# Expert loop: the scatter of an expert moved behind the first product of the next, the next expert's token rows moved ahead of the second product

## The reference

```
aff = softmax(h @ w_router)                       # 256 tokens x 16 experts
gate, idx = top_k(aff.T, 32)                      # each expert takes 32 tokens
xs = h[idx]                                       # (16, 32, 1024)
a = silu(xs @ w_gate) * (xs @ w_up)               # each 1024 x 1024 for an expert
out = (a @ w_down) * gate                         # 1024 x 1024
y = zeros(256, 1024).at[idx].add(out)             # added back at the tokens
```

## Time and profile before

| | |
|---|---|
| median of 3 runs | 2054.88 us (2052.83 to 2055.36) |
| profiled execution, its own time | 2058.72 us |
| span of the profiled execution | 2056.9 us |
| PE busy | 1718.2 us, 84% |
| DVE busy | 572.5 us, 28% |
| ACT busy | 416.4 us, 20% |
| moved from and to HBM | 571.73 MB, mean 278 GB/s |
| first expert stage (L1090 first to L1113 last) | 1042.0 to 1500.4 us |
| second expert stage | 1581.0 to 2038.9 us |

### The profile page before, as it was taken

One profiled execution on the slowest core, in us unless ns is written; L12 is line 12 of the kernel. 1 busy time (PEld: TensorE's weight loads), 2 busy tenths in 40 slices (PEclk: granted clock), 3 DMA queues, 4 the chain that ended last, 5 costly groups with the idle time before them and its releaser, 6 DMA issues.

```text
span 2056.9 us, 22697 instructions
## 1 busy us (share of the span) xinstructions
PE 1718.2 (84%) x9278; PEld 1084.1 (53%) x9278; DVE 572.5 (28%) x1298; ACT 416.4 (20%) x732; POOL 18.5 (1%) x26
## 2 busy tenths in 40 slices
PE   6999989999999999996878776776788886777776
PEld 4544348887888886553744333332345443343333
DVE  3243145116888536547230000000024000000002
ACT  4222241002130023212221111111123211111111
POOL 0000000000110000000000000000000000000000
PEclk8999997999999999887878889889897889889988
DMA  9425730244558835105379999999955999999995
GB/s 368 163 82 205 269 144 1 82 159 145 208 205 307 309 124 205 41 1 206 118 291 422 429 428 428 429 429 429 428 193 226 415 428 428 429 429 429 428 429 233
DMA packets 110591, 571.73 MB, mean 278 GB/s; under 512 B 9122, under 2 KB 15394, under 8 KB 85955
## 3 DMA queue, kind: packets, MB, share of 16 engines
q1 hardware_dynamic: 109488, 568.66, 68.5%
q10 hardware_dynamic: 1042, 2.24, 0.3%
HBM read 569.83 MB, written 1.05 MB: 278 GB/s over the span
## 4 chain that ended last, share of the span: by engine, by line
PE 58%; DMA 32%; DVE 5%; ACT 2%; issue 2%; SPq 1%; DVEq 0%; ACTq 0%
DMA ring<-in_w_exp_up_dram 29%; PE bank L456 19%; PE bank L1090 8%; PE bank L800 8%; PE bank L827 4%; PE bank L464 3%; PE bank L482 2%; PE bank L1152 1%; PE bank L1106 1%; PE bank L843 1%; PE bank L536 1%; DMA ring<-in_w_exp_down_dram 1%; PE bank L507 1%; PE bank L1113 1%; DMA ring<-in_w_ada_dram 1%
## 5 line engine op out<-in xcount | busy, mean ns | idle before, releaser
L1090 PE MATMUL bank<-ring,arena 128*32 128x512 f32 x2048 | 300.9, 743 | 101.7 <-DMA ring<-in_w_exp_up_dram 80.0
L1090 PEld LDWEIGHTS bank<-ring,arena 128*32 128x32 f32 x2048 | 80.7, 132 | 297.2 <-issue 243.0
L2289 DVE TENSOR_TENSOR arena<-arena,bank 128x256 f32<-128x256 f32 x32 | 13.5, 421 | 697.7 <-ACT arena L1580 697.7
L1106 PE MATMUL bank<-ring,arena 128*32 128x512 f32 x1024 | 134.3, 663 | 57.9 <-DVE arena L2289 49.2
L456 PE MATMUL bank<-ring,hT 128*128 128x512 f32 (+4 forms) x480 | 162.0, 494 | 6.5 <-issue 4.9
L800 PE MATMUL bank<-hT,ring 128*128 128x256 f32 x704 | 156.5, 385 | 4.2 <-ACT hT L1286 4.2
L800 PEld LDWEIGHTS bank<-hT,ring 128*128 128x128 f32 x704 | 135.4, 193 | 23.3 <-issue 4.6
L1113 PE MATMUL bank<-arena 128*128 (+1 forms) x512 | 118.9, 385 | 29.0 <-DVE arena L2293 29.0
L1113 PEld LDWEIGHTS bank<-arena 128*128 128x128 f32 x512 | 94.6, 190 | 69.5 <-issue 54.5
L456 PEld LDWEIGHTS bank<-ring,hT 128*128 128x128 f32 x480 | 87.5, 194 | 76.7 <-issue 66.9
L1076 PEld LDWEIGHTS bank<-arena 128*128 128x128 f32 x960 | 113.8, 194 | 1.6
(11 more groups left out here) (309 smaller groups left out, 1670.5 us busy)
## 6 DMA issues: line engine op xcount, KB each, us to landing
ring<-in_w_exp_gate_dram SPq DMA_DIRECT2D x64, 2048.0 KB, 17.6
ring<-in_w_exp_up_dram SPq DMA_DIRECT2D x64, 2048.0 KB, 22.1
ring<-in_w_exp_down_dram SPq DMA_DIRECT2D x64, 2048.0 KB, 22.4
ring<-in_w_mod_dram SPq DMA_DIRECT2D x24, 2048.0 KB, 13.5
ring<-in_w_ada_dram SPq DMA_DIRECT2D x12, 2048.0 KB, 13.3
ring<-in_w_up_dram SPq DMA_DIRECT2D x10, 2048.0 KB, 11.5
ring<-in_w_in_dram SPq DMA_DIRECT2D x8, 2048.0 KB, 14.1
ring<-in_w_down_dram SPq DMA_DIRECT2D x5, 2048.0 KB, 9.2
```

The lines of the kernel that those rows point to most:

```text
L1090: ins = pe.matmul(bank[0][32 * q:32 * q + 32, :], xe[:, k * CAP:(k + 1) * CAP], xs[q // 2][:, o:o + 512], start=(k == 0), stop=(k == KD - ...
L1106: ins = pe.matmul(bank[2 + h][32 * q:32 * q + 32, :], act_t[:, 4 * j + q, :], x[:, q, h * 512:h * 512 + 512], start=(j == 0), stop=(j == 1 ...
```

## The change

`down` is split in three: `products` (the four transposes), `down` (the down product) and `scatter`. The loop on PE is now `products(e)`, `rows(e + 1)`, `down(e)`, `gate_up(e + 1)`, `scatter(e)`. ACT's `between_products` is split in the same way, with the copy of the token rows ahead of the copy of bank 3. DVE and SP are as before, and so is the number of instructions of each kind.

```diff
-                def down(e, last=False):
+                def products(e):
+
                     pe.wait_ge(sem("gu_copied"), e + (N_EXP * layer + 1))
                     for j in range(4):
                         ins = pe.transpose(bank[1][:, j * 128:j * 128 + 128], gu[:, j * 128:j * 128 + 128], ident)
                     ins.then_inc(done, 1)
+
+                def down(e):
 
                     pe.wait_ge(sem("act_ready"), e + (N_EXP * layer + 1))
...
                     ins.then_inc(done, 1)
+
+                def scatter(e, last=False):
 
                     pe.wait_ge(sem("down_copied"), e * 2 + (2 * N_EXP * layer + 2))
...
                 with pe.Fori(0, N_EXP - 1) as e:
+                    products(e)
+                    rows(e + 1)
                     down(e)
-                    rows(e + 1)
                     gate_up(e + 1)
-                down(N_EXP - 1, last=True)
+                    scatter(e)
+                products(N_EXP - 1)
+                down(N_EXP - 1)
+                scatter(N_EXP - 1, last=True)
...
-                def between_products(e):
+                def gate_and_up(e):
                     act.wait_ge(sem("gate_up_done"), e * 2 + (2 * N_EXP * layer + 2))
...
+
+                def down_rows(e):
                     act.wait_ge(done, e * 3 + (base + 2))
                     act.copy(dsb[:, 1, :], bank[3]).then_inc(sem("down_copied"), 1)
...
                 with act.Fori(0, N_EXP - 1) as e:
-                    between_products(e)
+                    gate_and_up(e)
                     rows(e + 1)
-                between_products(N_EXP - 1)
+                    down_rows(e)
+                gate_and_up(N_EXP - 1)
+                down_rows(N_EXP - 1)
```

## The result

The changed kernel takes 2061.29 us (median of 7 runs, 2057.2 to 2064.46) against 2055.36 us for the kernel before on the same chip (7 runs, 2052.83 to 2056.44). The ratio is 1.0032 with a 95% interval of 1.0020 to 1.0044: slower by about 6 us. A second comparison, with 12 and 35 runs, gave 1.0030 (1.0017 to 1.0043). The forecast was 2054.4 us and no change, with a range that ended at 2060.

What follows compares the result with a forecast made beforehand. Transfers were taken to bound the expert loop, so only stage ends count: ramp -4.9, tails +4.7 (half clock) or +2.0 (full), branches +0.3, weighted about -0.6. Forecast median 2054.4 us, no change; range 2050.5 to 2060.

Steps and rivals of the forecast that it cites:

- Rivals 2 and 3: Inside the stages: slots, not bytes, set the period, 2032 us, chance 0.03; PE becomes the bound, +240 us, chance 0.01.
- the tail: Last landings to last scatter of each stage: scatter delays the last down product, +2.4 and +2.3 us at half clock.
- half clock at its start, 5.00 us: Tail: last gate/up half starts at half clock after a long wait and takes 5.00 us, against 3.64 at full clock.
- the ramp: Each stage's start, where PE hands back the first slots: hole before second slot 0 closes, -2.7 and -2.2, together -4.9 us.
- It just makes it; I count 0: Ramp: slot 4 goes out at 1065.7 to 1067.2, due by 1067.4; cost 0, with 0.5 us as bad end.
- rival 1: Ramp: the dry queue only moves to slot 4, token rows and down product at half clock; +11, 2066 us; chance 0.04.
- PE's path to the hand-back: Ramp, expert 0: from transposes' end at 1058.34, token rows to 1062.0, down product 3.64 to 5.15 us, end 1065.6 to 1067.1.
- The deadline: Ramp: slot 4 must land at 1055.6 + 4 x 4.9 = 1075.2, so be out by 1067.4.
- by bytes, 4.0 at the least: Ramp gain counted by bytes: first hole 2.0 us, the second scaled the same way, -4.0 us at the least.
- six pitches: Inside the stages: a pitch is one 2048 KB slot's transfer, 4.90 us at 428 GB/s; six slots, one expert, take 29.4 us.
- The alternative with the skill's 6.9 us: Ramp: a lone slot landing 6.9 us after issue would make holes of 1.0 and 1.2 us, a gain of 2.2.
- its cover in the steady expert: Steady expert: slots 4 and 5 handed back 4 to 5 us later, 12 us of cover left, so 0 us.

Runs made afterwards that it cites:

- e6: The change in rounds 1 to 13, first and last rounds with token rows behind down product and scatter between gate/up halves; 2051.95 against 2054.61 us before, ratio 0.9986.
- e5: The change plus five extra matmuls between the gate/up halves in each loop round; 2058.14 against 2054.61 us for the kernel before, ratio 1.0020.
- e8: The change plus two extra matmuls in PE's short waits ahead of the loop; 2057.26 against 2054.61 us for the kernel before, ratio 1.0006.
- e7: The changed kernel itself measured again, nothing altered; 2061.62 against 2054.61 us for the kernel before, ratio 1.0030.
- e3: The change, but the round ending with the last gate/up has the scatter ahead of it; 2059.74 against 2056.23 us for the kernel before, ratio 1.0012.
- e2: The change's scatter move alone, token rows back behind the down product and ACT's copies in old order; 2057.38 against 2056.23 us before, ratio 0.9997.
- e4: Against the kernel before: scatter moved between the gate/up halves, token rows behind the down product as before; 2051.48 against 2056.23 us, ratio 0.9978.
- e9: The change plus extra matmuls both ahead of the loop (two) and between the gate/up halves (five); ratio 0.9989 against the kernel before.

## Why the prediction was wrong

**Right:** that the transfers bind the middle, and that the ends decide. 352.4 us before and after between the same two landings, and e6, where thirteen rounds in the new order cost next to nothing. Rivals 2 and 3 (slots set the period; PE becomes the bound) are out: the rate stayed at 427 and 428 GB/s at a granted clock of 0.86 and 0.88.

**Right in kind, short in size: the tail.** Forecast +5.0 in the two stages; +6.4 in the first profile (14.9 and 14.8), +4.6 in the second (13.9 and 14.0). The step "half clock at its start, 5.00 us" took the two values shown in the earlier trace rows as the price of a long wait. The last half took 5.2 to 6.3 us in the two profiles. e5 splits the first profile's 14.9 into 12.3 with a warm half and 2.6 of clock. The rule of the Trainium skill cited in the prediction ("TensorE: Matmul & The Clock Gate", Loop structure matters more than you think), that a long wait for a DMA ahead of matmuls leaves them on a cold engine, agrees with both: 5.2 to 6.3 us behind waits of 4.5 to 6.1 us, and 3.64 with the wait filled. The length of a shorter wait did not decide it, as I had read from the earlier trace rows: in the changed kernel a gate/up half took 3.64 us behind a wait of 2.90 (at 1472.54) and 5.34 behind one of 2.93 (at 2015.39).

**Wrong: the ramp.** The failed step is the sentence on slot 4, "It just makes it; I count 0". Slot 4 went out at 20.9 us, and with it slot 5 landed 2.3 and 2.4 us later than before. It was rival 1, which had 0.04 and asked for 2 us of lateness to count as slower; 1.1 were enough. Three things in the step were off:

- PE's path to the hand-back. I had 7.3 to 8.8 us from the end of the transposes to the end of the down product, taking the 5.15 of L1106 as the whole dip of the clock. It was 10.3: the token rows took 5.33 and the down product 5.22. The wait of 1.58 us that the new order covers was paid for by some 3.3 us of slower work, counted against full clock, of which the down product's 1.6 are no more than the kernel before paid at that place (5.15). e8 shows the clock as the cause: with it held, both take their short times and slot 4 goes out at 17.7.
- The deadline. I had slot 4 due 7.8 us after its issue, the time of a DMA into an empty queue. Issued 2.1 and 2.5 us before slot 3 landed, it took 9.6 and 9.1. In the first stage it was 1.1 us late by my deadline and landed 2.9 late. With the Trainium skill's 2.0 us of fixed cost ("DMA: Bandwidth & Descriptors", Anatomy of one DMA, there for DMAs issued by GpSimd) the estimate for one slot is 6.9 us, further off still: this trace has 8.0 in an empty queue and 9.6 here.
- The price. It is set by the landing, not by the issue alone. With slot 4 out at 15.8 to 17.7 us, slot 5 lands at 32.9 to 33.4 and sooner is worth nothing. At 20.9 to 21.0 it lands at 34.1 to 36.1, since the same issue time brought landings 8.3 to 10.2 us later (e7 and e3, first stages). At 23.7 to 23.8, when the queue has run empty, slot 4 takes 7.6 to 7.9 us and slot 5 lands at 37.3 to 37.7. From there to the last landing nothing more is lost or won (401.4 to 401.9 us). The change stands in the second group in three of its four ramps and in the third in one.

**Right in kind, too large: the gain of the ramp.** It was there to be had. e2 and e4 reach 434.3 to 435.0 against 436.3 and 435.8, 2.7 and 2.9 us in the two stages together, where the sum had 4.9 and, by bytes, 4.0 at the least (scaled as the text says, that is 3.6). The 4.9 counted every microsecond that the second slot 0 was behind six pitches from the first landing. But slot 4 landed at 27.9 us or later in every ramp, also where it was issued at 15.8, and not at the 27.4 of the sum; no order here takes that back. By the medians e4 is 4.5 us under before with an unchanged tail, so with one profile of before the size stays open between 2.7 and 4.5. In the first profile of the change the ramp is 6.4 us worse than forecast: slot 5 lands 4.7 us later in the two stages together, and the closed hole gives back 3.2 instead of 4.9. The alternative with the skill's 6.9 us was worked out wrongly: with 6.9 for both landings the holes are 31.3 and 31.4 less 29.4 us, 1.9 and 2.0, and not 1.0 and 1.2.

e8 is 5 us under the change by ratio. In the change the token rows in front of the down product gave the gain away. Their move was costed at nothing for its cover in the steady expert, which is right there; in the first round the same move stands on the path to a transfer, and there I checked it with lengths at a clock that the move itself changed.

Open: why the clock is down at the transposes already in some ramps (slot 4 out at 23.8; in e5 the token rows took 6.88 us and the down product 6.12) and falls only in the token rows in others (20.9). What decides between them the runs don't show. Nor is it shown how the extra 0.5 to 2.4 us of a DMA issued shortly before the queue runs empty come about; no run varied the issue alone.

## What to carry to other kernels

In this loop, bound by transfers, the steady round hid every order that was tried; price a reordering there at the first hand-back of each buffer and at what follows the last landing. Put work that nothing waits for into the wait for data itself (the scatter between the two halves: 4.5 us faster), not behind it, where it delays the end, and not in front of the work that frees a buffer. Before counting a covered wait as a gain, look at the clock of the rows around it: here the short waits turned into fewer long ones, and the granted clock of the stages fell from 0.90 and 0.89 to 0.86 and 0.88.

## What the runs showed of the hardware

The clock fell while PE was busy without a break. In the changed kernel PE works from 1100.47 on with no idle time, behind a wait of 3.94 us, and the down product behind the token rows still takes 5.34 us:

```profile
1104.04 3.72 PE L1118 MATMUL bank<-arena 128*128 x16
1107.60 0.60 PE L1099 MATMUL bank<-cst,arena 128*128 128x128 f32 x4
1108.04 3.66 PE L1076 MATMUL bank<-arena 128*128 x32
1111.62 5.34 PE L1109 MATMUL bank<-ring,arena 128*32 128x512 f32 x32
```

```profile
1110.00:1112.00 2.00, 2.00 (x20) 1.74 (x23) 0.00 (x0) 0.27 (x1) 0.00 (x0) 1.00 1.06 451
1112.00:1114.00 2.00, 2.00 (x16) 0.58 (x12) 0.00 (x0) 0.10 (x1) 0.00 (x0) 0.54 0.94 401
```

The granted clock went from 1.00 to 0.54 just behind the token rows, 32 matmul instructions that stream 32 columns each. A busy column in the profile is no sign that the clock will hold. In other rounds the same sequence kept it (3.64 us at 2008.82, shown above).

Two 128x512 matmuls per stage, in waits of 0.8 and 1.2 us, kept some 6.8 us of half clock away in three of the four ramps of e8 and e9.

Slot 4, a DMA of 2 MB, landed 7.6 to 7.9 us after an issue into an empty queue (the four ramps with 23.7 or 23.8); the first DMAs of the stages took 7.7 to 8.6. Issued some 2 us before slot 3 landed, when slot 3 alone was still under way, it took 8.3 to 10.2 us (the nine ramps with 20.9 or 21.0).
